# An RWKV-7 and attention stack on one core: early decay products, gate blocks inside the group norm's wait, two output blocks side by side

## The chip, the cores and the metric

The kernel runs on one core of one Trainium2 chip, in one launch. The time is device microseconds of one execution. The kernel before was run three times: median 2448.25 us, from 2446.24 to 2455.63.

## What is computed

Two transformer blocks over 512 tokens of width 1024. The change touches only the first layer, RWKV-7 time mixing, which in the reference is this:

```python
rkv = jnp.einsum('pbtd,pde->pbte', jnp.stack([x_r, x_k, x_v]), w_rkv)
r, k, v = rkv[0], rkv[1], rkv[2]
w = -jax.nn.softplus(-(w0 + jnp.tanh(x_w @ w1) @ w2)) - 0.5
decay = jnp.exp(-jnp.exp(w.astype(f32)))
a = jax.nn.sigmoid(a0 + (x_a @ a1) @ a2)
g = jax.nn.sigmoid(x_g @ g1) @ g2
kk = to_heads((k * k_k).astype(f32))
kk = kk / jnp.maximum(jnp.linalg.norm(kk, axis=-1, keepdims=True), 1e-12)
k = k * (1.0 + (a - 1.0) * k_a)
...
# a scan over the tokens with r, decay, k, v, kk and kk * a gives y
...
mean = jnp.mean(y, axis=-1, keepdims=True)
var = jnp.mean(jnp.square(y - mean), axis=-1, keepdims=True)
y = (y - mean) * lax.rsqrt(var + GN_EPS)
y = y.reshape(B, T, D) * lnx_w.astype(f32) + lnx_b.astype(f32)
bonus = jnp.sum(r_h * k_h * r_k.astype(f32), axis=-1, keepdims=True) * v_h
y = (y + bonus.reshape(B, T, D)).astype(h.dtype) * g
return y @ w_o
```

After it come an MLP, a forgetting-attention layer, a second MLP, and a second block with sparse attention, a convolution and a third MLP. None of these is edited.

## The kernel before

**Tiling.** Activations lie transposed, as 8 tiles of 128 features x 512 tokens. Weights come as blocks of 128 x 1024 in one stream (raw, four buffers). GpSimd (POOL) splits each block into a rounded high part and a remainder (whi, wlo, two slots each); a product is three matmuls, high x high, high x low and low x high, so a block is 8 x 3 = 24 matmuls of 128 x 512. There is no scheduler: each engine's program is written out by hand, and semaphores order the engines. The semaphore blk counts the weight blocks that TensorE is through with, split_ready those that POOL has split. POOL splits block b as soon as blk reaches b - 1.

**Preparation of the scan.** TensorE computes k, r and v in blocks 6 to 29. After each of the first v blocks e stands a group of head sums (BETWEEN: the norm of kk after e = 0 and 1, the bonus sums "bo" two by two after e = 2 to 5), and after e = 3 to 6 two matmuls kk_spread, which spread the inverse norms (rows kkR) over the features. VectorE (DVE) makes the products in place: the bonus product r * r_k * k into tmpA and tmpB in turn (L1902), then, for each tile, the normed kk (L1919), kk * a (L1920) times the inverse decay RD (L1921), kk times the shifted decay (L1924), r times the decay DEC (L1930), k times RD (L1931). ScalarE (ACT) reads the v blocks and turns them over. Then TensorE transposes k, b = kk * a and v (tokens, L706), and matmuls L743 spread the bonus sums. The scan itself runs in 4 turns of 128 tokens and is bound to the engines' mutual waits.

**Group norm, gates and output.** When the scan is done, TensorE takes the means (L1001), DVE subtracts them (L2064), ACT squares (L1539), TensorE sums the squares by head (head_sum, L618), ACT takes the root and DVE the inverse (L2013, L2016, L1906). Only then begins a loop over 8 tiles e: a matmul spreads the inverse deviation (L631), 6 matmuls make the gate tile from sgH and sgL with the two gate_up blocks, DVE multiplies (L2069), ACT applies lnx_w and lnx_b (L1544), DVE adds the bonus BON (L2073), multiplies with the gate in PSUM (L2080), ACT rounds to YH (L1547), DVE subtracts to YL (L2084). After the loop, linear("rwkv_o") computes 8 output blocks of 24 matmuls; the first waits tile by tile for y_lo. The blocks of rwkv_o come after the two gate_up blocks in the stream, so POOL splits the first of them when gate tile 7 has released its slot. The stream itself stops before rwkv_o until the scan is done, since X is loaded again first (rec_done).

The lines at the places that the change touches:

```python
for e in range(DT):
    spread("gn", e, [2, 3], gnR)
    if e >= 2:
        pe.wait_ge(S("y_gated"), e - 1)
    mm = three(ps[:, 6 + e % 2, :], (g0 % SPL, e), sgH[:, 0, :], sgL[:, 0, :], True, False)
```

## Time and profile before

| what | value |
|---|---|
| median of three runs | 2448.25 us |
| the profiled execution: its own time | 2456.9 us |
| its span (first to last instruction) | 2455.1 us |
| TensorE busy | 2356.1 us (96%) |
| VectorE busy | 1185.8 us (48%) |
| ScalarE busy | 573.3 us (23%) |
| GpSimd busy | 1288.6 us (52%) |
| mean granted TensorE clock | 0.975 |

The profiled execution took 1.8 us more than its span, and 8.65 us more than the median of the runs. Time on the trace counts from the span's start. The preparation of the scan that the change rewrites lies at 153 to 252 us, the group norm, gates and output at 448 to 548 us. PE in a row is TensorE's matmul, DVE VectorE, ACT ScalarE, POOL GpSimd. KR in a row is one tensor that holds both r (Rr) and kk (KN), ps is PSUM, ssq also the scan's state; tmpA and tmpB are the two work tiles. A granted clock of 1.00 is 2.4 GHz, 0.50 is 1.2 GHz.

### The profile page before, as it was taken

The numbers are of one execution on the slowest core, as the hardware profiler recorded it, in microseconds if no ns is written. First come the engines' busy times: TensorE is split into PE (matmuls) and PEld (weight loads), VectorE is DVE, ScalarE is ACT, GpSimd is POOL, SyncE is SP. The second block draws the span as 40 slices with busy tenths as digits, with TensorE's granted clock in tenths as the row PEclk, the third lists the DMA queues.
The fourth block names the chain that finished last, engine by engine and source line by source line (L and its number), as shares of the span: only waits on it lengthen the run. The fifth ranks groups of instructions, "written<-read, shape, count | busy, mean of one in ns | idle before, by whom it ended". The sixth has DMA issues, their size and how long they took to land.

```text
span 2455.1 us, 41848 instructions
## 1 busy us (share of the span) xinstructions
PE 2356.1 (96%) x16922; PEld 1886.6 (77%) x16922; DVE 1185.8 (48%) x1476; ACT 573.3 (23%) x1168; POOL 1288.6 (52%) x839
## 2 busy tenths in 40 slices
PE   8998999899999999989999999999999998999999
PEld 5765888578888877667788888787877777888887
DVE  8857433474343462566544333518045656633433
ACT  4542333221110122144311011101015541201100
POOL 5642001066666665455566666566645445666665
PEclk9998999789999999999999999999999989999999
DMA  4220000122222222200222322233221112222322
GB/s 152 86 69 18 3 3 3 70 77 95 96 101 94 94 91 75 82 27 34 71 95 95 102 94 94 89 100 126 95 79 44 44 35 69 95 95 96 101 94 86
DMA packets 50447, 188.37 MB, mean 77 GB/s; under 512 B 5616, under 2 KB 5744, under 8 KB 49808
## 3 DMA queue, kind: packets, MB, share of 16 engines
q1 hardware_dynamic: 49824, 183.40, 22.3%
q10 hardware_dynamic: 496, 3.12, 0.3%
q8 instruction: 99, 1.62, 0.3%
q14 instruction: 28, 0.23, 0.0%
HBM read 184.33 MB, written 2.10 MB: 76 GB/s over the span
## 4 chain that ended last, share of the span: by engine, by line
PE 85%; DVE 10%; issue 2%; ACT 1%; POOL 1%; DMA 0%; ACTq 0%; DVEq 0%; SPq 0%; POOLq 0%
PE ps L606 23%; PE ps L608 22%; PE ps L607 22%; PE ps L1109 2%; PE ps L1124 2%; PE ps L793 2%; PE ps L618 2%; DVE HL L1993 1%; PE ps L1090 1%; PE ps L803 1%; PE ps L1091 1%; PE ps L801 1%; PE ps L786 1%; PE ps L779 1%; PE ps L631 1%
## 5 line engine op out<-in xcount | busy, mean ns | idle before, releaser
L448 POOL TENSOR_TENSOR wlo<-raw,whi 128x1024 fp32r<-128x1024 f32 (+1 forms) x354 | 825.6, 2332 | 26.4
L441 POOL TENSOR_SCALAR whi<-raw 128x1024 fp32r<-128x1024 f32 x335 | 361.1, 1078 | 808.6 <-PE ps L608 796.5
L606 PE MATMUL ps<-HH,whi 128*128 128x512 f32 x1312 | 529.8, 404 | 8.3 <-DVE HL L1993 8.3
L608 PE MATMUL ps<-HH,wlo 128*128 128x512 f32 x1312 | 514.4, 392 | 0.0
L607 PE MATMUL ps<-HL,whi 128*128 128x512 f32 x1312 | 514.1, 392 | 0.0
L606 PEld LDWEIGHTS ps<-HH,whi 128*128 128x128 f32 x1312 | 248.2, 189 | 70.0 <-DVE HL L1993 14.1
L607 PE MATMUL ps<-hidL,whi 128*128 128x512 f32 x768 | 298.8, 389 | 0.0
L606 PE MATMUL ps<-hidH,whi 128*128 128x512 f32 x768 | 298.8, 389 | 0.0
L608 PE MATMUL ps<-hidH,wlo 128*128 128x512 f32 x768 | 298.8, 389 | 0.0
L608 PEld LDWEIGHTS ps<-HH,wlo 128*128 128x128 f32 x1312 | 248.3, 189 | 52.8
L607 PEld LDWEIGHTS ps<-HL,whi 128*128 128x128 f32 x1312 | 248.6, 190 | 52.2 <-issue 4.3
L2040 DVE TENSOR_TENSOR X<-X,ps 128x512 f32<-128x512 f32 x192 | 123.3, 683 | 306.7 <-PE ps L608 306.7
L1511 ACT ACTIVATE sqrT<-relT 128x512 f32<-128x512 f32 x96 | 60.8, 634 | 792.0 <-DVE relT L2029 792.0
L2032 DVE TENSOR_TENSOR hidL<-sqrT,hidH 128x512 fp32r<-128x512 f32 x96 | 184.1, 1936 | 88.8 <-ACT hidH L1515 88.8
L2029 DVE SCALAR_TENSOR_TENSOR relT<-ps,rstd 128x512 f32<-128x512 f32 x96 | 66.4, 691 | 234.1 <-PE ps L608 234.0
L606 PEld LDWEIGHTS ps<-hidH,whi 128*128 128x128 f32 x768 | 144.2, 188 | 29.9
L607 PEld LDWEIGHTS ps<-hidL,whi 128*128 128x128 f32 x768 | 144.2, 188 | 29.9
L608 PEld LDWEIGHTS ps<-hidH,wlo 128*128 128x128 f32 x768 | 144.2, 188 | 29.8
L478 POOL TENSOR_TENSOR mRB<-mRB,cst 128x512 f32<-128x512 f32 x8 | 10.1, 1279 | 174.3 <-ACT mRB L1465 174.3
L507 POOL TENSOR_SCALAR prs<-prs,cls,GT 128x32 f32<-128x32 f32 (+4 forms) x48 | 32.9, 686 | 79.7 <-DVE cls L2167 67.8
L606 PE MATMUL ps<-mixH,whi 128*128 128x512 f32 x128 | 52.4, 409 | 10.8 <-DVE mixL L1849 8.8
L1335 ACT ACTIVATE HH<-X,vec 128x512 fp32r<-128x512 f32 x40 | 28.8, 721 | 143.1 <-DVE X L2000 70.3
(445 smaller groups left out, 3598.4 us busy)
## 6 DMA issues: line engine op xcount, KB each, us to landing
raw<-stream SPq DMA_DIRECT2D x336, 512.0 KB, 3.3
X<-xT SPq DMA_DIRECT2D x2, 1024.0 KB, 6.7
X<-xT SPq DMA_DIRECT2D x1, 2048.0 KB, 7.9
CW<-cmpw ACTq DMA_DIRECT2D x1, 2048.0 KB, 9.5
out<-X SPq DMA_DIRECT2D x4, 512.0 KB, 2.7
cst<-consts SPq DMA_DIRECT2D x1, 511.5 KB, 9.3
c2f<-consts ACTq DMA_DIRECT2D x1, 466.0 KB, 3.0
c2s<-consts ACTq DMA_DIRECT2D x1, 466.0 KB, 4.1
```

The source lines that it names most:

```text
L441: pool.tensor_scalar(hi, raw[:, j, :].rearrange("p (k m) -> p k m", k=DT), 1.0, 0.0, ALU.mult, ALU.add)\
L448: return pool.tensor_tensor(wlo[:, s, a:z, :], raw[:, j, a * P:z * P].rearrange("p (k m) -> p k m", k=z - a), whi[:, s, a:z, :].bitcast(F3 ...
L606: pe.matmul(acc, whi[:, s, k, :], hi, start=start, stop=False)
L607: pe.matmul(acc, whi[:, s, k, :], lo, start=False, stop=False)
L608: return pe.matmul(acc, wlo[:, s, k, :], hi, start=False, stop=stop)
L618: pe.matmul(ps[0:112, bank, :], gather_heads(i), tmp[i % 2][:, :], start=i == 0, stop=i == n - 1).then_inc(S(f"{tag}_sum"), 1)
L793: mm = pe.matmul(square(hp, 1 - c, hp, p), mN[half(c), hp, p, :], mT[half(c), hp, p, :], start=True, stop=True)
L1109: mm = pe.transpose(ps[0:w, 4 + hp, j * P:(j + 1) * P], B["P"][:, 2 * (u % 2) + hp, j * P:j * P + w], ident)
L1511: act.activation(sqrT[:, j % 2, :], relT[:, j % 2, :], ACT.Square).then_inc(S("full"), 1)
L2029: dve.scalar_tensor_tensor(relT[:, j % 2, :], ps[:, j, :], 0.0, rstd[:, :], ALU.max, ALU.mult).then_inc(S("rel"), 1)
L2032: dve.tensor_tensor(hidL[buf][:, j - 1, :], sqrT[:, (j - 1) % 2, :], hidH[buf][:, j - 1, :].bitcast(F32), ALU.subtract).then_inc(S("hid"), 1)
L2040: ins = dve.tensor_tensor(X[:, e, :], X[:, e, :], ps[:, 4 + 2 * (j % 2) + o, :], ALU.add)
```

## The change

Three parts.

**Early decay products.** A new buffer bon holds the bonus products of tiles 0 to 5 (6 and 7 go to tmpA and tmpB), so they need not wait for the head sums before them. A function decayed(i) makes, as soon as tile i of r is read, the bonus product, -a * RD, r * DEC and k * RD; tiles 0 to 5 stand ahead of the inverse norms of kk, tiles 6 and 7 behind them. The sign of kk moves into k_k. Of the loop over kk_spread three operations for each tile stay. ACT's first copy of the turned tokens also waits for kn.

**Group norm and gates.** lnx_b is added to BON by ACT during the scan (two tiles at the start of each turn). Means use four banks and alternate with head sums. Gate tiles 0 to 4 stand directly behind the head sums, ahead of the first spread; ACT copies each gate tile to a new buffer G in SBUF. DVE applies lnx_w together with the inverse deviation, so that ACT's affine step goes. DVE's y_lo moves ahead of the bonus sum.

**Two output blocks side by side.** Blocks 0 and 1 of rwkv_o are split into buffers of their own (oH, oL, in the place of kk), from the end of the scan on. TensorE takes them together, tile by tile: as soon as y_lo of tile k is there, 6 matmuls (y_apart). Gate tiles 5 to 7 and spreads 3 to 7 stand between them. Blocks 2 to 7 follow.

```diff
-                if not isinstance(b, int) or b >= 2 * RAW:
+                if not isinstance(b, int) or b >= 2 * RAW and not 0 <= b - START["rwkv_o"] < 4:
                     pool.wait_ge(S("blk"), b - (SPL - 1))
+                elif b - START["rwkv_o"] in (0, 1):
+                    pool.wait_ge(S("rec_done"), 1)
+                elif b - START["rwkv_o"] in (2, 3):
+                    pool.wait_ge(S("blk"), START["rwkv_o"])
...
+            pe.wait_ge(S("y_done"), NCH)
+            for i in range(DT + 3):
+                if i < DT:
+                    if i >= 4:
+                        pe.wait_ge(S("gn_c"), i - 3)
+                    pe.matmul(ps[:, i % 4, :], const("bones"), Rr[:, i, :], start=True, stop=True).then_inc(S("gn_mean"), 1)
+                if i >= 3:
+                    head_sum("gn", i - 3, DT)
...
+            def y_apart(e, k):
+
+                acc = ps[:, e, :]
+                pe.matmul(acc, oH[:, e, k, :], YH[:, k, :], start=k == 0, stop=False)
+                pe.matmul(acc, oH[:, e, k, :], YL[:, k, :], start=False, stop=False)
+                mm = pe.matmul(acc, oL[:, e, k, :], YH[:, k, :], start=False, stop=k == DT - 1)
+                if k == DT - 1:
+                    mm.then_inc(S("blk"), 1)
+
+            SPREADS = [2, 3, 5]
+            for e in range(5):
+                gate_tile(e)
+            pe.wait_ge(S("gn_c"), DT)
+            for i in range(3):
+                spread("gn", i, SPREADS, gnR)
+            for k in range(DT):
+                if k + 5 < DT:
+                    gate_tile(k + 5)
+                if k + 3 < DT:
+                    spread("gn", k + 3, SPREADS, gnR)
+                if k == 0:
+                    ready(y0 + 1)
+                pe.wait_ge(S("y_lo"), k + 1)
+                for e in range(2):
+                    y_apart(e, k)
...
             for n in range(QT):
+                act.wait_ge(S("bo_used"), DT)
+                for i in (2 * n, 2 * n + 1):
+                    mark(act.activation(BON[:, i, :], BON[:, i, :], ACT.Identity, bias=vcol("lnx_b", i)), "bias_added")
...
+            for e in range(5):
+                gate_read(e)
+            for i in range(DT):
+                if i + 5 < DT:
+                    gate_read(i + 5)
+                act.wait_ge(S("y_gated"), i + 1)
+                mark(act.activation(YH[:, i, :], tmp[i % 2][:, :], ACT.Copy), "y_hi")
...
+            def decayed(i):
+                dve.wait_ge(S("rkv_read"), 8 + i + 1)
+                product = bon[:, i, :] if i < 6 else tmp[i - 6][:, :]
+                mark(dve.scalar_tensor_tensor(product, Rr[:, i, :], vcol("r_k", i), Kk[:, i, :], ALU.mult, ALU.mult), "bo_sq")
+                mark(dve.scalar_tensor_tensor(AG[:, i, :], AG[:, i, :], -1.0, RD[:, i, :], ALU.mult, ALU.mult), "kn_rest")
+                dve.wait_ge(S("bo_sq"), i + 1)
+                mark(dve.tensor_tensor(Rr[:, i, :], Rr[:, i, :], DEC[:, i, :], ALU.mult), "rt")
+                mark(dve.tensor_tensor(Kk[:, i, :], Kk[:, i, :], RD[:, i, :], ALU.mult), "kt")
...
-            bonus(0)
-            bonus(1)
+            for i in range(6):
+                decayed(i)
             dve.wait_ge(S("kk_norm"), 1)
...
-            bonus(2)
-            bonus(3)
+            decayed(6)
+            decayed(7)
             for i in range(DT):
                 dve.wait_ge(S("kk_spread"), i + 1)
                 link(dve.tensor_tensor(KN[:, i, :], KN[:, i, :], ps[:, 6 + i % 2, :], ALU.mult), "kk_used")
-                link(dve.tensor_tensor(AG[:, i, :], AG[:, i, :], KN[:, i, :], ALU.mult))
-                mark(dve.tensor_tensor(AG[:, i, :], AG[:, i, :], RD[:, i, :], ALU.mult), "bt")
+                dve.wait_ge(S("kn_rest"), i + 1)
+                mark(dve.tensor_tensor(AG[:, i, :], AG[:, i, :], KN[:, i, :], ALU.mult), "bt")
...
+                dve.wait_ge(S("bt"), i + 1)
+                mark(dve.tensor_tensor(a[:, :, 1:C], a[:, :, 1:C], d[:, :, 0:C - 1], ALU.mult), "kn")
...
+            dve.wait_ge(S("gn_c"), DT)
+            dve.wait_ge(*count("bias_added", DT))
             for n in range(DT + 2):
                 if n < DT:
                     dve.wait_ge(*count("gn_spread", n + 1))
-                    mark(dve.tensor_tensor(Rr[:, n, :], Rr[:, n, :], ps[:, 2 + n % 2, :], ALU.mult), "gn_used")
...
+                    mark(dve.scalar_tensor_tensor(Rr[:, n, :], Rr[:, n, :], vcol("lnx_w", n), ps[:, (2, 3, 5)[n % 3], :], ALU.mult, ALU.mult), "gn_used")
```

On DVE, ahead of the inverse norms of kk, before the change. Rows name line, operation, output and inputs, width, and the semaphores waited for; kk_norm is the root of the norms by ACT:

```order
98 L1902 SCALAR_TENSOR_TENSOR tmpA<-KR,vec,Kk 128x512 [waits kk_sum,dve_chain]
99 L1902 SCALAR_TENSOR_TENSOR tmpB<-KR,vec,Kk 128x512 [waits kk_sum]
100 L1911 TENSOR_SCALAR rstd<-rstd 112x512 [waits kk_norm]
101 L1912 RECIPROCAL rstd<-rstd 112x512 [waits dve_chain]
102 L1913 CAST kkR<-rstd 112x512 [waits dve_chain]
```

The same place of the changed kernel, from the last of the six early tiles on:

```order
118 L1976 TENSOR_TENSOR Kk<-Kk,RD 128x512
119 L1972 SCALAR_TENSOR_TENSOR bon<-KR,vec,Kk 128x512 [waits rkv_read]
120 L1973 SCALAR_TENSOR_TENSOR AG<-AG,RD 128x512
121 L1975 TENSOR_TENSOR KR<-KR,DEC 128x512 [waits bo_sq]
122 L1976 TENSOR_TENSOR Kk<-Kk,RD 128x512
123 L1985 TENSOR_SCALAR rstd<-rstd 112x512 [waits kk_norm]
124 L1986 RECIPROCAL rstd<-rstd 112x512 [waits dve_chain]
125 L1987 CAST kkR<-rstd 112x512 [waits dve_chain]
```

24 operations on whole tiles now stand between the copy of the decays and the inverse norms, where two stood, and they wait for the reads of r, not for sums.

On TensorE, behind the head sums of the group norm, before (heads_root is the inverse deviation, heads_sq a square):

```order
1569 L618 MATMUL ps<-tmpB,cst 112x512 [waits heads_sq]
1570 L631 MATMUL ps<-gnR,pselR 128x512 [waits heads_root,sg_split,split_ready]
1571 L606 MATMUL ps<-sgH,whi 128x512
1572 L607 MATMUL ps<-sgL,whi 128x512
1573 L608 MATMUL ps<-sgH,wlo 128x512
```

And in the changed kernel, the end of gate tile 4 and what follows:

```order
1598 L623 MATMUL ps<-sgH,whi 128x512
1599 L624 MATMUL ps<-sgL,whi 128x512
1600 L625 MATMUL ps<-sgH,wlo 128x512
1601 L648 MATMUL ps<-gnR,pselR 128x512 [waits heads_root,gn_c]
1602 L648 MATMUL ps<-gnR,pselR 128x512 x2
1603 L623 MATMUL ps<-sgH,whi 128x512 [waits gn_aff]
...
1609 L648 MATMUL ps<-gnR,pselR 128x512 [waits heads_used]
1610 L1045 MATMUL ps<-YH,oH 128x512 [waits y_lo,split_ready]
1611 L1046 MATMUL ps<-YL,oH 128x512
1612 L1047 MATMUL ps<-YH,oL 128x512
```

30 gate matmuls (1571 to 1600) moved ahead of the wait for the inverse deviation, and the output matmuls for tile 0 now stand behind gate tile 5, ahead of gate tiles 6 and 7.

On DVE, one step of the gated output before, and then one step of the changed kernel:

```order
231 L2069 TENSOR_TENSOR KR<-KR,ps 128x512 [waits heads_spread]
232 L2073 TENSOR_TENSOR KR<-KR,BON 128x512 [waits gn_aff]
233 L2080 TENSOR_TENSOR tmpA<-KR,ps 128x512 [waits y_hi,gate_up,dve_chain]
234 L2084 TENSOR_TENSOR YL<-tmpB,YH 128x512 [waits y_hi]
```

```order
229 L2139 SCALAR_TENSOR_TENSOR KR<-KR,vec,ps 128x512 [waits heads_spread]
230 L2143 TENSOR_TENSOR YL<-tmpB,YH 128x512 [waits y_hi]
231 L2147 TENSOR_TENSOR KR<-KR,BON 128x512 [waits heads_used]
232 L2151 TENSOR_TENSOR tmpA<-KR,G 128x512 [waits y_lo,gn_aff,dve_chain]
```

Four operations stay four. The sum with BON no longer waits for ACT, the gate comes from SBUF (G) where it came from PSUM, and gn_aff is now ACT's copy of the gate tile.

## Rows read from the trace of the kernel before

**Rows 1.** The page: the chain of work that ended last, by engine.

```profile
PE 85%; DVE 10%; issue 2%; ACT 1%; POOL 1%; DMA 0%; ACTq 0%; DVEq 0%; SPq 0%; POOLq 0%
```

**Rows 2.** Waits of TensorE, 150 to 560 us: total us, times, longest.

```profile
PE ps L631 <- DVE gnR L1906: 6.2, 1, 6.2
PE ps L618 <- DVE tmpB L1902: 5.1, 1, 5.1
PE ps L706 <- DVE boR L1906: 4.7, 1, 4.7
```

**Rows 3.** Stretches: length, busy us of PE, PEld, DVE, ACT, POOL; granted clock; DMA.

```profile
200.00:205.00 5.00, 1.89 (x2) 0.45 (x2) 4.86 (x7) 0.00 (x0) 1.18 (x1) 0.51 0.01 3
...
455.00:460.00 5.00, 5.00 (x12) 1.72 (x12) 1.99 (x3) 1.56 (x3) 0.00 (x0) 1.00 0.95 387
...
465.00:470.00 5.00, 0.00 (x0) 0.00 (x0) 4.89 (x4) 0.00 (x0) 0.00 (x0) 0.64 0.00 0
...
480.00:498.00 18.00, 18.00 (x36) 10.55 (x36) 12.99 (x21) 7.21 (x10) 0.00 (x0) 0.50 0.00 1
```

**Rows 4.** Timeline of TensorE, v blocks: start, us, idle before it.

```profile
197.01 1.02 PE L618 MATMUL ps<-tmpA,cst 128*112 128x512 f32 x2
203.11 2.05 PE L618 MATMUL ps<-tmpB,cst 128*112 128x512 f32 x2 [5.08 <-DVE tmpB L1902]
...
234.25 5.35 PE L706 MATMUL ps<-cst,Kk 128*128 128x128 f32 x32 [4.68 <-DVE boR L1906]
...
243.11 0.49 PE L743 MATMUL ps<-boR,pselR 48*128 48x512 f32 x1
```

**Rows 5.** Timeline of VectorE, the same stage.

```profile
176.56 0.75 DVE L1902 SCALAR_TENSOR_TENSOR tmpA<-KR,vec,Kk 128x512 f32<-128x512 f32 x1 [16.92 <-PE ps L618]
...
182.20 4.35 DVE L1906 TENSOR_TENSOR kkR<-rstd,kkR 16x512 fp32r<-16x512 f32 x2
...
199.01 2.71 DVE L1921 TENSOR_TENSOR AG<-AG,RD 128x512 f32<-128x512 f32 x1
...
232.74 1.41 DVE L1906 TENSOR_TENSOR boR<-ps,boR 16x512 fp32r<-16x512 f32 x2
```

**Rows 6.** Timeline of GpSimd: one split.

```profile
197.40 1.04 POOL L441 TENSOR_SCALAR whi<-raw 128x1024 fp32r<-128x1024 f32 x1 [4.52 <-PE ps L608]
198.52 2.65 POOL L448 TENSOR_TENSOR wlo<-raw,whi 128x1024 fp32r<-128x1024 f32 x1
```

**Rows 7.** Timeline of ScalarE: reads of r, copies of the turned tokens.

```profile
153.56 5.38 ACT L1381 ACTIVATE KR<-ps 128x512 f32<-128x512 f32 x8 [1.01 <-PE ps L608]
...
240.29 4.08 ACT L1452 ACTIVATE Btok<-ps 128x512 f32<-128x512 f32 x8
```

**Rows 8.** Timeline of TensorE: group norm, gates, output, start of the MLP.

```profile
463.23 1.02 PE L618 MATMUL ps<-tmpB,cst 128*112 128x512 f32 x2
470.40 0.76 PE L631 MATMUL ps<-gnR,pselR 48*128 48x512 f32 x1 [6.15 <-DVE gnR L1906]
...
477.52 0.79 PE L631 MATMUL ps<-gnR,pselR 48*128 48x512 f32 x1
...
501.96 0.77 PE L606 MATMUL ps<-YH,whi 128*128 128x512 f32 x1 [2.88 <-issue]
...
510.05 0.39 PE L606 MATMUL ps<-YH,whi 128*128 128x512 f32 x1
...
548.13 0.39 PE L606 MATMUL ps<-HH,whi 128*128 128x512 f32 x1
```

**Rows 9.** Timeline of VectorE: steps of the gated output, and its last row.

```profile
478.36 0.69 DVE L2069 TENSOR_TENSOR KR<-KR,ps 128x512 f32<-128x512 f32 x1 [1.57 <-PE ps L631]
478.96 0.68 DVE L2073 TENSOR_TENSOR KR<-KR,BON 128x512 f32<-128x512 f32 x1
...
480.28 0.68 DVE L2084 TENSOR_TENSOR YL<-tmpA,YH 128x512 fp32r<-128x512 f32 x1
...
503.82 2.79 DVE L2084 TENSOR_TENSOR YL<-tmpB,YH 128x512 fp32r<-128x512 f32 x1
```

More of the change, by code:

```diff
@@ L993, in mlp @@
                 down(base + 60, 7, 1, last=True)
-            g0 = START["gate_up"]
-            for i in range(DT):
-                pe.wait_ge(S("y_done"), NCH)
-                if i >= 2:
-                    pe.wait_ge(S("gn_c"), i - 1)
-                pe.matmul(ps[:, i % 2, :], const("bones"), Rr[:, i, :], start=True, stop=True).then_inc(S("gn_mean"), 1)
-            head_sums("gn", DT)
-            ready(g0 + 1)
-            pe.wait_ge(S("sg_split"), 1)
-            for e in range(DT):
-                spread("gn", e, [2, 3], gnR)
-                if e >= 2:
-                    pe.wait_ge(S("y_gated"), e - 1)
-                mm = three(ps[:, 6 + e % 2, :], (g0 % SPL, e), sgH[:, 0, :], sgL[:, 0, :], True, False)
+            pe.wait_ge(S("y_done"), NCH)
@@ L1016, in _ @@
+            pe.wait_ge(*count("gn_used", DT))
+            for e in range(2, DT):
+                ready(y0 + e)
+                if e >= 4:
+                    pe.wait_ge(S("x_up"), e - 3)
+                for k in range(DT):
+                    mm = three(ps[:, e % 4, :], ((y0 + e) % SPL, k), YH[:, k, :], YL[:, k, :], k == 0, k == DT - 1)
+                mm.then_inc(S("blk"), 1)
             mlp(0, 1, HH, HL)
```

97 lines of the change are left out of this document (53 added, 44 removed).

## The prediction, on record before the changed kernel ran

> **What bounds the kernel now.** I read the chain of waits first: 85% of it is TensorE [rows 1], so most of the kernel is matmul after matmul and this change cannot touch it. The list of TensorE's waits then shows where the first layer is not: three waits of 6.2, 5.1 and 4.7 us, all for VectorE, and all in the two stretches that the diff rewrites [rows 2]. The table of stretches adds a second loss: the granted clock is 0.51 around the 5.1 us wait, falls to 0.64 in the 6.15 us one, and is 0.50 through the whole gate loop [rows 3], though TensorE there shows as busy 18.00 of 18.00 us. So each long wait is paid twice, as a wait and as matmuls at 1.2 GHz behind it. The reader should see from the timelines that in the v blocks TensorE waits for a product that VectorE could have made long before (VectorE idled 16.92 us ahead of 176.56, though r was being read from 153.56 on) [rows 5, 7], and that in the gate loop every tile costs (477.52 - 470.40) / 2 = 3.56 us [rows 8].
>
> **First part, the preparation.** On TensorE from 197.01 to 234.25 stand three v blocks, four bonus sums, six spreads, and the waits [rows 4]. A block of 24 matmuls at full clock takes (548.13 - 510.05) / 7 = 5.44 us [rows 8], three are 16.3; a bonus sum is about 0.88 (its row says 1.02 for a pair of matmuls that overlaps the next by its drain [rows 4]), four are 3.5; six spreads at 0.36, my estimate from the 0.49 of such a row, are 2.2. Sum 22.0, so without waits the transposes start at 219.05, not at 234.25: 15.2 us less. That needs VectorE to be in time at two places.
>
> The inverse norms of kk come first. VectorE now has 24 tile operations ahead of them. It starts at about 154.3, when the first tile of r is read [rows 7]. A tile operation takes about 0.64 us from start to start (the rows at 478.36 and 478.96 stand 0.60 apart, a scalar_tensor_tensor is 0.75 long) [rows 5, 9], together 15.3. But the same rows show that an operation whose inputs both lie in SBUF waits for a POOL operation under way: 2.71 us at 199.01, until 0.55 after POOL's end at 201.17, and 4.35 for two small rows at 182.20 [rows 5, 6]. All 24 are of that kind. Four splits of 1.04 + 2.39 us fall into this stretch (the second half is 2.65 when one VectorE operation slips in between [rows 6]). Walking them through in turn, I get 3 to 4 operations between the first splits, 8 in the long gap up to 173, and the last done at 181.3. The inverse (0.42 + 3.35 + 0.43 + two small rows of 0.70, about 5.8 us with its links) ends at 187.1. TensorE asks for it after v block 3 and two sums, which is one block and two spreads ahead of 197.01 [rows 4], at 190.8. Slack 3.7 us, so I cost the move at nothing; without that cover each microsecond late would be one of TensorE's. The second place is the loop over kk_spread: three operations for a tile, about 2.05 us, where five to eight stood, so that VectorE is through with tile 7 at 217.6 and with the bonus rows (1.41) [rows 5] at 219.0, just when TensorE ends its last v block. The 4.7 us wait goes; what is late next is nothing by more than 0.2 us.
>
> The transposes: 64 of them took 243.11 - 234.25 = 8.86 us [rows 4], the first 32 at a clock that was still recovering. Then ACT's copies bound them, 4.08 / 8 = 0.51 us each [rows 7]. The last v read ends at 220.1 (219.05, 0.4 of drain, one copy), TensorE's last group follows the twelfth copy, 220.1 + 12 x 0.51 + 0.6 = 226.8; so 7.7 us from 219.05, a further 1.2 gained. Everything up to the scan is paced as before. ACT's new wait for kn (217.6) holds only that first copy, which is later anyway. First part: **-16.4 us**; bounds -17.5 (the copies start with the transposes) and -11 (one lock more on the way, a wait of some 3 us and half clock behind it).
>
> The two bias activations at the head of each turn of the scan are 0.5 to 0.7 us each by the nearest ACT passes over a tile [rows 7]. I cost them at nothing: ACT waits there for VectorE's masking of the first products. Without that cover the copy to mRB is late, at the worst by 1.4 us in three turns.
>
> **Second part, group norm and gates.** Means and sums are 16 products of about 0.88 us. Before, with two banks, the last sum began at 463.23 [rows 8]; interleaved from 447.83 on with one short wait for the first square, it ends at 462.2 instead of 464.25: -2.0. The chain root, inverse, cast and rows stays 6.15 us long, so the inverse deviation is there at 468.3. Gate tiles 0 to 4, 6 matmuls of 0.227 us each (5.44 / 24) or 1.36 us a tile, fill 462.1 to 468.9. The wait of 6.2 us is covered, and with it the reason for the low clock: tiles cost 1.36 where the loop took 3.56.
>
> Then VectorE paces. A step is 2.53 us of its own time (478.36 to 480.28 plus 0.61) [rows 9] and about 2.7 with the wait for ACT's rounding. But for tiles 0, 1 and 2 there is a ring: gate tile k+5 on TensorE, ACT's copy of it, which stands ahead of ACT's rounding of tile k, VectorE's y_lo, y_apart, the next gate tile: 1.36 + 0.4 + 0.6 + 0.6 + 0.75 + 1.36, about 5 us. That gives y_lo of tile 0 at 473.4 and tile 1 at 478.4. At 481.4 gate tile 7 is done and blk reaches 32: POOL now splits blocks 34 and 35, 6.9 us of locks, in the middle of the steps. VectorE's sum, gate product and y_lo all read two SBUF tensors; before, the gate came from PSUM, and POOL came only at the last steps (2.79 us at 503.82 [rows 9]). I get y_lo of tile 2 at 485.3 and of tile 3 at 491.1, then 2.73 each, tile 7 at 502.1, y_apart done at 503.5.
>
> The Trainium skill, page "SBUF — State Buffer", section "Who interferes with whom", says that a VectorE instruction with two SBUF inputs contends with a GpSimd instruction that reads SBUF and that the loser fully blocks; by it the new gate operand is a cost, and without it the sum would be 4 us better. The 2.71 and 2.79 us rows agree with it.
>
> Blocks 32 and 33 cost POOL nothing on the path: the X load and the stream keep the DMA queues at 0.95 until 460 [rows 3], POOL splits them by 465 to 467, and they are asked for at 472. Blocks 2 to 7 are 6 x 5.44 = 32.7 us: the MLP starts at 536.2 instead of 548.13 [rows 8]. Second and third part: **-11.9 us**, bounds -16.5 (no lock in steps 2 and 3) and -7.
>
> **Sum.** -16.4 - 11.9 = -28.3 us. The profiled execution took 2456.9 (span 2455.1) and would take 2428.6; the median lies 8.65 below it, at 2448.25, so the forecast is 2420.
>
> **The rivals.**
> Clock falls again. TensorE idles about 3.9 us ahead of y_lo 2, and 3.9 again ahead of y_lo 3. Waits of 4.68 and 5.08 us had half clock behind them [rows 3, 4]; none of 3.9 is there to read. If it falls, steps stay paced by VectorE (2.6 us of matmuls in 2.73), but the last y_apart takes 1.3 more, and blocks 2 on start at half clock, as the first output block did before: 510.05 - 501.96 = 8.1 instead of 5.44, so 2.6. Together +3.9: 2424.
> The Trainium skill, page "TensorE: Matmul & The Clock Gate", section "HAM oscillation — how this bites in real kernels", describes this: bursts with waits between them, each starting throttled. It speaks for this rival.
> The locks miss. POOL and VectorE ask within 0.1 us of each other ahead of y_lo 2; if VectorE gets in first, steps 2 and 3 gain about 4 us and TensorE never idles long: 2416.
> Inverse norms late. If the 24 operations meet the locks worse, by more than 3.7 us, TensorE waits ahead of v block 4, some 3 us plus 3 of half clock, and the loop behind slips: +6 to +8, 2427. For it: 24 operations against 8 POOL instructions. Against: the 16.92 us of idleness that they go into.
> The output blocks gain nothing. If y_lo keeps the old 3.56 us pace, tile 7 comes at 507 to 508 and the last term is worth 5 us less: 2425.
> Slower than before. The clock falls at 482 and does not recover in the run of output blocks. 24 matmuls at half clock last 10.3 us (0.43 each), six blocks cost 29 more, with the 1.3 above about +30.5: 2450. It decides from 5.6 blocks at half clock on. Before, the first output block took 8.1 us where half clock throughout would be 10.3, so the clock came back within it, which speaks against this rival.
>
> **How the numbers follow.** A measurement of this kernel can tell about 0.5% (12.2 us) from no change. Chances: forecast 0.40, clock falls 0.24, locks miss 0.10, inverse norms late 0.12, old pace 0.07, slower rival 0.02, and 0.05 for what I have not seen, spread over all sides. The cases from 2416 to 2427, each some 4 us wide because the runs before lie within 9.4 us, give 2412 to 2431. Faster by over 0.5% (below 2436): 0.93; within: 0.05; slower: 0.02.
>
> **What would show it.** In the profile after: no wait of TensorE over 1 us between 165 and 235, clock 1.00 there; transposes starting near 219; the scan starting at 236; kk's inverse norms before 190.8. Later, 16 us earlier than the times above: gate tiles right behind the last sum at clock 1.00; y_lo of tile 2 up to 2.4 us long; two TensorE waits of about 4 us for YL; the MLP starting near 520. I am wrong if a wait for kkR stands ahead of v block 4, or if the six output blocks take over 36 us.

## The result, and the profile after

| kernel | median us | lowest to highest | executions |
|---|---|---|---|
| before | 2447.67 | 2446.24 to 2455.63 | 4 |
| changed | 2427.66 | 2425.18 to 2428.23 | 4 |

The ratio is 0.9911, 95% interval 0.9893 to 0.9929: 20.0 us less, faster by more than the 0.5% that this measurement can tell from no change. The profiled execution of the changed kernel took 2427.87 us with a span of 2426.0, which is 29.1 less than the span of before. These two differences, 20.0 and 29.1, are the first thing to explain, and the stages are the way to do it.

The list of TensorE's waits from 140 to 560 us, in the form of [rows 2], now reads so:

```profile
PE ps L1045 <- DVE YL L2143: 10.2, 5, 4.9
PE ps L789 <- issue: 2.2, 3, 1.6
PE ps L623 <- DVE mixL L1919: 2.0, 1, 2.0
```

The three waits of [rows 2] are gone. What stands in their place is one group for YL, five waits with 10.2 us together, the longest 4.9. The chain of the page, beside [rows 1]:

```profile
PE 87%; DVE 8%; issue 2%; ACT 2%; POOL 1%; DMA 0%; ACTq 0%; DVEq 0%; SPq 0%; POOLq 0%
```

VectorE's share fell from 10 to 8%. The timeline of TensorE in the preparation, beside [rows 4]:

```profile
164.93 1.02 PE L635 MATMUL ps<-tmpA,cst 128*112 128x512 f32 x2
...
190.33 1.88 PE L635 MATMUL ps<-bon,cst 128*112 128x512 f32 x4
192.14 0.72 PE L731 MATMUL ps<-kkR,pselR 48*128 48x512 f32 x2
...
220.79 3.68 PE L723 MATMUL ps<-cst,Kk 128*128 128x128 f32 x32
...
228.17 0.49 PE L763 MATMUL ps<-boR,pselR 48*128 48x512 f32 x1
...
237.16 1.98 PE L799 MATMUL ps<-KR,AG 64*64 64x128 f32 x64 [0.84 <-issue]
```

No row of this stretch carries a wait for VectorE. The transposes start at 220.79 where they started at 234.25. The first 32 take 3.68 us where they took 5.35, so the clock is up when they begin, as the stretches say:

```profile
165.00:190.00 25.00, 25.00 (x92) 16.41 (x91) 24.83 (x25) 7.25 (x11) 12.79 (x6) 1.00 0.26 84
190.00:205.00 15.00, 15.00 (x57) 9.96 (x56) 14.76 (x16) 1.20 (x2) 8.05 (x4) 1.00 0.10 37
205.00:235.00 30.00, 30.00 (x161) 22.10 (x161) 18.41 (x28) 11.91 (x23) 3.79 (x2) 1.00 0.00 1
```

TensorE is busy for 70.00 of 70.00 us at a granted clock of 1.00 (its upper level). In the first of these stretches VectorE is busy for 24.83 of 25.00 us, where it worked for 11.26 of them before. Its timeline, beside [rows 5]:

```profile
155.62 2.88 DVE L1972 SCALAR_TENSOR_TENSOR bon<-KR,vec,Kk 128x512 f32<-128x512 f32 x1 [2.25 <-ACT KR L1440]
...
180.90 0.68 DVE L1976 TENSOR_TENSOR Kk<-Kk,RD 128x512 f32<-128x512 f32 x1
...
181.96 3.35 DVE L1986 RECIPROCAL rstd<-rstd 112x512 f32<-112x512 f32 x1
185.34 1.99 DVE L1987 CAST kkR<-rstd 112x512 fp32r<-112x512 f32 x1
187.36 1.40 DVE L1980 TENSOR_TENSOR kkR<-rstd,kkR 16x512 fp32r<-16x512 f32 x2
```

The 24 early operations end at 181.5, the inverse norms at 188.76. TensorE asks for them at 192.14: they are 3.4 us early.

In the output, TensorE's timeline beside [rows 8]:

```profile
433.39 3.70 PE L1021 MATMUL ps<-KR,cst 128*128 128x512 f32 x8 [0.69 <-ACT KR L1551]
...
446.80 1.02 PE L635 MATMUL ps<-tmpB,cst 128*112 128x512 f32 x2
...
454.60 0.96 PE L648 MATMUL ps<-gnR,pselR 48*128 48x512 f32 x3
...
464.40 0.50 PE L1045 MATMUL ps<-YH,oH 128*128 128x512 f32 x1 [1.51 <-DVE YL L2143]
...
465.97 0.63 PE L623 MATMUL ps<-sgH,whi 128*128 128x512 f32 x1
...
477.65 0.80 PE L1045 MATMUL ps<-YH,oH 128*128 128x512 f32 x1 [4.91 <-DVE YL L2143]
...
522.64 0.39 PE L623 MATMUL ps<-HH,whi 128*128 128x512 f32 x1
```

The old 6.15 us wait ahead of the first spread is filled with gate tiles. The waits have moved into the steps: the longest are 1.51 us ahead of 464.40 and 4.91 ahead of 477.65; the other three are 1.96, 1.26 and 0.57 us. The stretches show what the clock made of them:

```profile
446.00:456.00 10.00, 10.00 (x39) 6.98 (x40) 5.91 (x6) 4.31 (x7) 3.71 (x3) 1.00 0.33 105
456.00:466.00 10.00, 6.53 (x26) 4.39 (x26) 7.54 (x12) 2.34 (x4) 0.00 (x0) 0.99 0.01 2
466.00:472.00 6.00, 4.74 (x14) 2.95 (x12) 2.42 (x3) 1.12 (x2) 2.96 (x2) 0.73 0.00 0
472.00:478.00 6.00, 1.09 (x4) 0.53 (x3) 5.92 (x5) 0.63 (x1) 4.96 (x3) 0.84 0.26 87
478.00:486.00 8.00, 8.00 (x18) 5.56 (x18) 7.13 (x12) 1.89 (x3) 0.00 (x0) 0.50 0.18 66
486.00:492.00 6.00, 5.43 (x23) 4.14 (x22) 3.97 (x7) 2.34 (x4) 0.00 (x0) 0.98 0.00 0
```

The five gate tiles ahead of the first spread run at 1.00. The clock falls a first time behind the waits of 1.96 and 1.51 us: the matmul at 465.97 takes 0.63 us where it took 0.39, and the mean over 466 to 472 is 0.73. From 478 to 486 the clock is 0.50, its lower level, and it is back at 0.98 behind. What TensorE waits for is in VectorE's timeline, beside [rows 9]:

```profile
458.66 0.69 DVE L2143 TENSOR_TENSOR YL<-tmpA,YH 128x512 fp32r<-128x512 f32 x1
...
463.65 0.69 DVE L2143 TENSOR_TENSOR YL<-tmpB,YH 128x512 fp32r<-128x512 f32 x1 [2.32 <-ACT YH L1617]
...
469.92 0.69 DVE L2143 TENSOR_TENSOR YL<-tmpA,YH 128x512 fp32r<-128x512 f32 x1 [3.58 <-ACT YH L1617]
470.53 2.87 DVE L2147 TENSOR_TENSOR KR<-KR,BON 128x512 f32<-128x512 f32 x1
...
475.54 2.06 DVE L2143 TENSOR_TENSOR YL<-tmpB,YH 128x512 fp32r<-128x512 f32 x1
...
487.76 0.69 DVE L2143 TENSOR_TENSOR YL<-tmpB,YH 128x512 fp32r<-128x512 f32 x1 [0.70 <-ACT YH L1617]
```

Two things stretch the steps. First, VectorE waits 2.32 and 3.58 us for ACT's rounding, and ACT itself had been waiting for a gate tile:

```profile
462.51 0.60 ACT L1609 ACTIVATE G<-ps 128x512 f32<-128x512 f32 x1 [3.88 <-PE ps L625]
463.00 0.62 ACT L1617 ACTIVATE YH<-tmpB 128x512 fp32r<-128x512 f32 x1
```

This is the ring of the prediction: TensorE makes gate tile 6 behind the output matmuls of step 0, ACT copies it before it rounds tile 1, and step 1 of TensorE needs that rounding. Second, a sum takes 2.87 us instead of 0.68 and a y_lo 2.06 instead of 0.69, while GpSimd splits two blocks (these waits of VectorE for GpSimd are called locks here):

```profile
468.96 1.05 POOL L454 TENSOR_SCALAR whi<-raw 128x1024 fp32r<-128x1024 f32 x1 [19.17 <-PE ps L625]
470.09 2.76 POOL L461 TENSOR_TENSOR wlo<-raw,whi 128x1024 fp32r<-128x1024 f32 x1
```

**The difference by stage.** The preparation goes from the first head sum of kk to the scan's first matmul, the output from the first mean to the first matmul of the MLP. For the profiled execution of before the borders are 163.59, 252.11, 447.83 and 548.13.

| kernel | first sum at | preparation | scan | output | rest | span |
|---|---|---|---|---|---|---|
| before | 163.59 | 88.52 | 195.72 | 100.30 | 1906.97 | 2455.1 |
| changed | 164.93 | 72.23 | 196.23 | 89.25 | 1903.36 | 2426.0 |
| difference | +1.34 | -16.29 | +0.51 | -11.05 | -3.61 | -29.1 |

The two stages that the diff edits give 27.34 of the 29.1 us. The rest, behind the MLP's start, is 3.61 us shorter, though the change doesn't touch it; the later first sum and the scan take 1.85 back.

### The profile page after: what moved, and what is told of

It is laid out like the page before. It is cut to its first block, busy times and chain, and to the rows that moved or that the text cites. A ratio compares the mean times of both kernels' runs of the same rounds, so it can differ in the third digit from the quotient of the medians.

```text
span 2426.0 us, 41845 instructions
## 1 busy us (share of the span) xinstructions
PE 2339.6 (96%) x16922; PEld 1878.7 (77%) x16922; DVE 1190.7 (49%) x1469; ACT 576.1 (24%) x1176; POOL 1293.8 (53%) x839
## 4 chain that ended last, share of the span: by engine, by line
PE 87%; DVE 8%; issue 2%; ACT 2%; POOL 1%; DMA 0%; ACTq 0%; DVEq 0%; SPq 0%; POOLq 0%
PE ps L623 23%; PE ps L624 23%; PE ps L625 23%; PE ps L1168 2%; PE ps L1183 2%; PE ps L813 2%; PE ps L635 2%; DVE HL L2061 1%; PE ps L1149 1%; PE ps L1150 1%; PE ps L823 1%; PE ps L821 1%; PE ps L806 1%; DVE ssq L1845 1%; PE ps L799 1%
```

## The experiments

Twelve kernels ran, in three groups of four, each group on one chip beside the kernel before, which ran 17, 9 and 8 times there: medians 2453.37, 2453.45 and 2453.50. Each ratio is to the runs of the same group. The changed kernel itself ran only in the first group (after_again), so the later kernels are compared with it across chips. Stage lengths come from one profiled execution of each kernel. Excerpts of diffs are against the changed kernel, and dots mark what is left out.

### The two kernels again

**before_again** and **after_again** are the two kernels with no edit.

> The kernel before, unchanged, to settle why the profiled execution took 29 us less after the change (span 2455.1 to 2426.0) and the medians only 20 us less. Theory: the profiled execution of before was a long one; its stage from 153 to 548 us is ordinary, and the surplus lies in stretches at half clock behind it. Then this profile shows the first MLP starting within 1.5 us of 548.1, a span near 2446, and about 5 us less of half-clock cost after 548. Rival: the stage itself was long in that execution; then the MLP starts near 542.5 here and the rest is as long as before (1907 us). Time: 2447, ratio 1.000.

> The changed kernel, unchanged. Theory: the MLP starts at 522.6 within 1.5 us, and what is behind it lasts 1903 us within 4, where half clock falls elsewhere from execution to execution. Rival: what is behind the MLP's start is steadily 5 us longer than in the kernel before, because other phases of the clock meet other waits. Time 2427, 20 us less than before.

Before: 2453.37 (2446.90 to 2458.22, 12 executions), ratio 1.0002, 0.9988 to 1.0015. Changed: 2429.85 (2429.34 to 2430.36), ratio 0.9902, 0.9888 to 0.9917. So before has a spread of 12 us, and a median of three can lie anywhere in it: of the 17 executions beside this job, 4 took 2446.2 to 2448.6, at a granted clock over the whole span of 0.981 or 0.982, the other 13 took 2452 to 2459. Of the 34 executions of the three groups, 7 took under 2449 us; of the four behind the result above, 3 did. Their low median was thus in good part luck, though that their chip had a share in it isn't excluded. Where in the program the short executions save their time wasn't seen: the two profiled ones of before took 2456.9 and 2452.51 us. The forecast of 2447 for before_again leaned on the low median and was a miss. By stage the profile of before_again has 88.45, 196.65, 100.00 and a rest of 1902.07, after_again 72.21, 195.86, 91.00 and 1905.26. The edited stages repeat within 0.3 us in before and differ by 1.8 in the output of the changed kernel, which the part on the ring comes back to. The rest differs by 4.9 us between two executions of before alone, and over all 14 profiles, whatever the edit, it lies between 1901.1 and 1907.3. In the second pair it is 3.19 us longer in the changed kernel where it was 3.61 shorter in the first. So the 3.61 us above are within what executions differ by, and no sign of the change.

The first sum comes 0.74 to 1.34 us later in the two profiles of the changed kernel, and the stretch from 140 to 160 us shows a companion of it. First before_again, then after_again:

```profile
140.00:160.00 20.00, 18.01 (x80) 14.49 (x79) 12.79 (x13) 11.42 (x19) 10.43 (x7) 1.00 0.22 79
```

```profile
140.00:160.00 20.00, 18.01 (x73) 14.44 (x72) 16.71 (x18) 10.76 (x18) 8.76 (x6) 0.91 0.22 78
```

The same wait of 2.0 us for mixL stands in both, the busy time is the same 18.01, yet the clock is 1.00 in one and 0.91 in the other. Of the 14 profiles seven have 0.91 here and seven 1.00. The kernel with the output edits alone has 0.91, and four kernels of the sections below that do have the early products have 1.00 (round_first, early_splits, filled_wait and four_side_by_side, all on one chip), so the change doesn't decide it. The first sum comes at 163.94 to 165.05 with 0.91 and at 162.81 to 164.13 with 1.00. What decides the clock here stays open.

### One part at a time

**prep_only** keeps the early products and the order of the head sums, with group norm, gates and output as before. **output_only** is the converse: group norm, gates, bias activations and output as changed, the products and the order of the head sums as before.

```diff
 # prep_only
-            for i in range(DT + 3):
-                if i < DT:
-                    ...
-                if i >= 3:
-                    head_sum("gn", i - 3, DT)
...
+            for i in range(DT):
+                ...
+            head_sums("gn", DT)
...
+            linear("rwkv_o", YH, YL, ("y_lo", 0), ("x_up", 0), [])
 # output_only
-    bon = at("bon", [P, 6, T], zone(8, 4096))
...
-            def decayed(i):
...
```

> Only the first part: the early decay products, with bon, k_k negated and the shorter loop over kk_spread; group norm, gates and output as before. Theory: the part saves its 16.3 us of the trace, the scan starts at 236 to 237.5 and the MLP at 532; time 16 us less than before, 2431. Rival, that a good part of the traced gain does not arrive at the end (the medians moved by 20 and not 27): 11 to 12 us less, 2436.

> Only the second and third part: bias in the scan, four banks for the means, gate tiles ahead of the spreads, G in SBUF, output blocks 0 and 1 tile by tile; the preparation of the scan as before. Theory: from the first mean to the MLP's start 89.2 us where before has 100.3, the whole 11 us less, 2436. Rival, that the gain does not all arrive: 7 to 8 us less, 2440. The sum of this gain and that of the preparation alone should be that of the whole change within 4 us.

prep_only: 2438.20 (2437.05 to 2441.44), ratio 0.9940, 0.9927 to 0.9953, that is -15.2 us; preparation 72.23, output 100.04. output_only: 2442.82 (2441.38 to 2448.08), ratio 0.9957, 0.9944 to 0.9970, -10.6 us; preparation 88.71, output 91.13. Together -25.7, against -23.5 for both in one kernel: the parts add up within their intervals, and each acts in its own stage alone. The expected savings of 16 and 11 us came, and the times expected with them (2431 and 2436) were too low by the low median of before. The scan keeps its length, 196.61 in prep_only and 196.23 in the changed kernel with its bias activations: these cost nothing that shows.

### How far from late are the inverse norms

**late_kk_6** and **late_kk_12** put extra VectorE passes, whose result nothing reads, ahead of the inverse norms of kk.

```diff
+            for _ in range(6):
+                link(dve.tensor_tensor(ssq[:, :], RD[:, 0, :], DEC[:, 0, :], ALU.mult))
             dve.wait_ge(S("kk_norm"), 1)
```

> The changed kernel with 6 more VectorE passes (RD x DEC of tile 0 into a scratch tile, not read, linked one behind the other) ahead of the inverse norms of kk. Theory: the inverse norms are ready 3.4 us before TensorE asks for them (188.8 against 192.1). Six passes of 0.7 us and one lock more (about 2.8) make them 7 late, so TensorE waits 3 to 4 us ahead of v block 4, about 5 us with half clock behind it: 2434. Rival, that the slack is worth nothing to begin with or that the loop over kk_spread takes the delay up: 2429 or 2437.

> The same with 12 passes. Theory: the rows come 11 to 12 us later, TensorE waits 8 us ahead of v block 4 and works some microseconds at half clock: about 10 us over the changed kernel, 2439. That prices a preparation in which VectorE's early products meet too many locks. Rival: under 5 us, 2434, because the later waits of the preparation shrink by as much.

The passes of VectorE and the first spread of TensorE behind them, first with six, then with twelve:

```profile
180.80 7.11 DVE L1985 TENSOR_TENSOR ssq<-RD,DEC 128x512 f32<-128x512 f32 x6
...
191.79 1.93 DVE L1989 CAST kkR<-rstd 112x512 fp32r<-112x512 f32 x1
```

```profile
195.21 1.18 PE L731 MATMUL ps<-kkR,pselR 48*128 48x512 f32 x2 [3.75 <-DVE kkR L1980]
```

```profile
180.53 14.26 DVE L1985 TENSOR_TENSOR ssq<-RD,DEC 128x512 f32<-128x512 f32 x12
...
198.67 0.43 DVE L1989 CAST kkR<-rstd 112x512 fp32r<-112x512 f32 x1
```

```profile
200.58 1.22 PE L731 MATMUL ps<-kkR,pselR 48*128 48x512 f32 x2 [9.35 <-DVE kkR L1980]
```

7.11 less a slack of 3.4 is 3.7, and the wait is 3.75. 14.26 less 3.4 is 10.9, less the 1.5 that the cast no longer waits for GpSimd is 9.4, and the wait is 9.35. The slack is thus measured from the other side. The stage grows to 79.19 and 83.69, +7.0 and +11.5, that is the wait and some 3 or 2 us of half clock behind it: the granted clock from 190 to 205 is 0.77 and 0.66. The times are 2434.61 (2433.06 to 2437.27), ratio 0.9922, 0.9900 to 0.9944, and 2437.14 (2436.68 to 2443.62), ratio 0.9943, 0.9923 to 0.9962: 4.8 and 7.3 over after_again. The first was expected at 2434 and came; the second lies between its theory (2439) and its rival (2434). Why the medians grew less than the stages isn't settled; 2 to 4 us are within what executions differ by behind the MLP's start.

### The ring, the locks and the clock

**round_first** lets ACT round tile i before it copies gate tile i + 5. **early_splits** gives the output blocks 2 and 3 buffers of their own, loads them ahead of X, and lets GpSimd split them when the scan is done, so that no split falls into the steps. **filled_wait** puts 20 matmuls, whose result nothing reads, ahead of the wait of step 3.

```diff
 # round_first
-                if i + 5 < DT:
-                    gate_read(i + 5)
                 act.wait_ge(S("y_gated"), i + 1)
                 mark(act.activation(YH[:, i, :], ...), "y_hi")
+                if i + 5 < DT:
+                    gate_read(i + 5)
 # early_splits
+            APART[START["rwkv_o"] + 2 + e] = o2H[:, e, :, :], o2L[:, e, :, :]
...
+            rest(START["rwkv_o"], RAW)
             sp.wait_ge(S("rec_done"), 1)
...
-                elif b - START["rwkv_o"] in (0, 1):
+                elif b - START["rwkv_o"] in (0, 1, 2, 3):
                     pool.wait_ge(S("rec_done"), 1)
 # filled_wait
+                if k == 3:
+                    pe.wait_ge(S("gn_aff"), 8)
+                    for _ in range(20):
+                        pe.matmul(ps[:, 6, :], oH[:, 0, 0, :], YH[:, 0, :], start=True, stop=True)
                 pe.wait_ge(S("y_lo"), k + 1)
```

> The changed kernel with one edit: ACT rounds tile i to YH before it copies gate tile i+5, not after. Theory (the ring): y_lo of tiles 1 and 2 waits for gate tiles that TensorE makes only after the output matmuls of the tile before, so each of these steps costs 5 to 6 us instead of 2.7. Without the ring y_lo 1 and 2 come 2.7 to 3.2 us apart, POOL's two splits still fall into the steps behind, and from the first mean to the MLP's start it takes 85 us where the changed kernel takes 89 to 91: 5 us less than it, time 2425. Rival (the locks decide): the ring only moved the wait, the two splits come earlier and cost the same, gain under 2 us, 2428.

> The changed kernel with output blocks 2 and 3 also split into buffers of their own (zone 9), the four blocks loaded ahead of the X load and split from the end of the scan on; the ring stays, blocks 2 and 3 are still computed after 0 and 1. Theory (locks): no POOL work lies in the eight steps, so VectorE's operations of 2.87, 1.41 and 2.06 us go back to 0.7; y_lo 3 comes 4.5 us earlier, TensorE's wait of 4.9 us falls to 1.3 and the clock stays at 1.00: 84 us from the first mean to the MLP, 6 us less than the changed kernel, 2424. Rival: the splits now meet the chain of the inverse deviation (cast and two small rows) and cost there what they cost later, 2429.

> The changed kernel with 20 more matmuls (oH x YH into a free bank, not read) put into TensorE's longest wait, ahead of y_lo 3. Theory (clock): that wait of 4.9 us brings half clock, which costs 1.3 us on the last output tile and up to 2.6 on the block behind; filled, the clock stays 1.00 to the MLP and the stage ends 2 to 3 us earlier, 2427. Rival: VectorE paces the steps whatever the clock, and the clock is back before the last tile, so nothing moves: 2429 to 2430.

| kernel | median us | ratio, 95% | output stage |
|---|---|---|---|
| after_again | 2429.85 | 0.9902 (0.9888 to 0.9917) | 91.00 |
| round_first | 2420.81 | 0.9877 (0.9858 to 0.9897) | 83.71 |
| early_splits | 2421.51 | 0.9878 (0.9859 to 0.9897) | 85.19 |
| filled_wait | 2427.16 | 0.9903 (0.9886 to 0.9920) | 89.64 |

The executions of round_first (2418.34 to 2424.20) and early_splits (2420.56 to 2423.25) all lie below the eight of the changed kernel (2425.18 to 2430.36), though the intervals of the ratios touch. Without the ring, y_lo of tiles 0 to 3 start at 457.03, 459.75, 462.47 and 465.47, VectorE's own pace of 2.7 to 3.0 us apart, where they stood 5.0, 6.3 and 5.6 apart; the step behind is still 5.6 long, with a y_lo of 2.06 us: the locks. Without the locks, it is the other way round: the ring's steps of 6.4 and 5.0 us remain for tiles 0 to 2, and then all are 2.7. Against the 89.25 of the first profile the ring costs 5.5 us and the locks 4.1; against the 91.00 of the second 7.3 and 5.8.

The two profiles of the changed kernel differ just in the ring. From y_lo of tile 0 to that of tile 1 it takes 4.99 us in the first and 6.46 in the second, and TensorE's clock in this step makes the difference. The first profile, then after_again:

```profile
459.50:464.40 4.90, 3.39 (x13) 2.33 (x13) 2.55 (x5) 1.11 (x2) 0.00 (x0) 1.00 0.01 3
```

```profile
458.45:464.81 6.36, 4.86 (x13) 3.38 (x13) 2.54 (x5) 1.11 (x2) 0.00 (x0) 0.76 0.01 3
```

TensorE is busy for 1.47 us more, which is all of the difference: the 12 matmuls between one y_lo and the next, six of output and six of a gate tile, stand in the ring. The wait ahead of them is 1.96 us in both. The other kernels that keep ACT's order agree: a ring step takes 4.96 to 5.03 us where the clock is 1.00 and 6.27 to 6.60 where it is 0.73 to 0.77. The output stage goes with it, 89.25 to 89.64 us where the first ring step ran at 1.00 and 91.00 to 91.13 where it did not. So the short waits do cost through the clock, 1.3 to 1.6 us a ring step. The first profile and early_splits have one slow ring step each, so the 4.1 us of the locks compares like with like.

filled_wait kept the clock up where it was to, from 478 to 486, but not 10 us sooner. Its stretches:

```profile
466.00:472.00 6.00, 4.49 (x13) 2.74 (x12) 2.77 (x2) 1.11 (x2) 3.65 (x2) 0.78 0.00 0
...
478.00:486.00 8.00, 6.16 (x25) 4.02 (x24) 7.12 (x12) 1.90 (x3) 0.00 (x0) 1.00 0.12 50
```

With the clock at 1.00 instead of 0.50 in those 8 us the stage is 89.64, no shorter than 89.25. From y_lo of tile 3 to the MLP it takes 47.10 us in the first profile, 47.12 in after_again and 47.17 in filled_wait. TensorE was busy for 8.00 of them before and is for 6.16 now: VectorE sets the pace of these steps, and TensorE at half clock just keeps up. The half clock from 478 to 486 is a companion of the loss and not a cause; the low clock in the ring steps, ahead of the filled wait, this kernel didn't touch. Its time of 2427.16, though it is the 2427 of the theory, can't be told from that of after_again, and the stage went as the rival said.

### Both causes out, and four blocks side by side

**round_and_early** joins the first two. **four_side_by_side** has the early splits and computes output blocks 2 and 3 in the steps too, which leaves two PSUM banks for the gates and two for the spreads. **four_spreads_early** is the same with another order of VectorE's step, the sum first and the use of the spread last.

```diff
 # four_side_by_side, on top of early_splits and round_first
-            SPREADS = [2, 3, 5]
+            SPREADS = [4, 5]
...
-                if k + 3 < DT:
-                    spread("gn", k + 3, SPREADS, gnR)
+                if k + 2 < DT:
+                    spread("gn", k + 2, SPREADS, gnR)
...
                 pe.wait_ge(S("y_lo"), k + 1)
-                for e in range(2):
+                for e in range(4):
                     y_apart(e, k)
 # four_spreads_early, VectorE's turn n
 #   before: used(n), y_lo(n - 2), add(n - 1), gated(n - 1)
 #   now:    add(n - 1), y_lo(n - 2), gated(n - 1), used(n)
```

> Four output blocks side by side, with the early splits and ACT's rounding first; gates in banks 6 and 7, spreads in 4 and 5, output in 0 to 3; POOL splits blocks 4 and 5 behind gate tile 7. Theory: a step has 12 output matmuls, 2.72 us, as long as VectorE's 2.7, so TensorE never waits over 1 us and the clock stays 1.00; the steps take about 27 us from y_lo 0 and four blocks (21.8) remain: about 75 us from the first mean to the MLP where the changed kernel takes 89 to 91. Time 2415, 14 us less than the changed kernel, 38 less than before. Rival: the splits of blocks 4 and 5 fall into the steps and hold VectorE up by 5 us, 2420.

> Four output blocks side by side as before, but VectorE takes the sum with BON first, then y_lo of the tile before, the gate product, and the spread product last. In the first form each y_lo stood behind a spread product whose spread TensorE made only after the output matmuls of the step before, two banks being too few: steps of 5 to 8 us. Theory: now TensorE paces, 2.72 us of output matmuls, a spread (0.4) and in three steps a gate tile (1.36), about 28.5 us from y_lo 0 on, then four blocks: 77.5 us from the first mean to the MLP's start, where the changed kernel takes 89 to 91 and the first form 91.3. Time 2416. Rival: ACT's rounding and the two late splits hold the steps at 3.5 us or more, 81 us and 2419.

> Both edits on the changed kernel, two blocks side by side: ACT rounds first, and blocks 2 and 3 are split early into buffers of their own. Alone they took the stretch from the first mean to the MLP to 83.7 and 85.2 us from 89 to 91. Theory: ring and locks are two costs and add up, since with both gone nothing holds VectorE's steps of 2.7 us: 79.5 us, time 2417. Rival: they overlap, because the lock fell into a step that the ring stretched anyway: 83 us, 2420.

round_and_early: 2417.86 (2415.20 to 2419.66), ratio 0.9855, 0.9832 to 0.9879, the fastest of all. Its output stage is 79.41 and its clock 1.00 from 456 to 480 us. Against the first profile the two costs add up: 9.8 us from 89.25 with both gone, 5.5 and 4.1 one by one. Against the 91.00 of the second it is 11.6, and 7.3 and 5.8 one by one, so they add up within the 1.8 us by which the stage of one kernel differs. Its steps in VectorE's timeline:

```profile
458.75 0.69 DVE L2150 TENSOR_TENSOR YL<-tmpA,YH 128x512 fp32r<-128x512 f32 x1
461.46 0.69 DVE L2150 TENSOR_TENSOR YL<-tmpB,YH 128x512 fp32r<-128x512 f32 x1
...
478.01 0.69 DVE L2150 TENSOR_TENSOR YL<-tmpB,YH 128x512 fp32r<-128x512 f32 x1 [0.70 <-ACT YH L1622]
```

Seven steps take 19.3 us, 2.75 each, where the changed kernel's take 29.1.

four_side_by_side: 2427.96 (2425.76 to 2428.51), ratio 0.9899, 0.9880 to 0.9918, output stage 91.32. Expected were 2415 and a stage of 75 us, so this was a miss. The reason stands in VectorE's timeline:

```profile
464.70 0.75 DVE L2144 SCALAR_TENSOR_TENSOR KR<-KR,vec,ps 128x512 f32<-128x512 f32 x1 [5.20 <-PE ps L652]
...
472.57 0.75 DVE L2144 SCALAR_TENSOR_TENSOR KR<-KR,vec,ps 128x512 f32<-128x512 f32 x1 [5.19 <-PE ps L652]
```

With two spread banks in place of three, TensorE can write spread k + 2 only behind the output matmuls of step k - 1, and these wait for a y_lo that VectorE does after it has used a spread. With that order turned round, four_spreads_early takes 2419.60 (2416.13 to 2423.52), ratio 0.9858, 0.9834 to 0.9882, stage 81.75, as its rival said (81 us, 2419): most of the loss was this ring. Its stage is still 2.3 us longer than that of round_and_early, and the two times can't be told apart. Its y_lo come at 458.00, 460.71, 466.76, 471.51, 478.55. In the two steps from 460.71 on VectorE still waits 3.25 and 1.95 us for a spread, and in the one behind them GpSimd, which now splits blocks 4 and 5 from 469.77 to 477.96, stretches a y_lo to 2.76 us.

## Why the prediction came out as it did

**The stages came out as forecast, within 3 us.** The preparation was forecast at -16.4 us and gave -16.3 (-16.2 in the second pair). The output was forecast at -11.9 and gave -11.05 and -9.0. The steps, with the clock of before moved on to each stage's own start: transposes forecast at 219.05 + 1.34 = 220.4, seen at 220.79. The 24 operations done at 181.3 + 1.34 = 182.6, seen at 181.5. Inverse norms with a slack of 3.7, seen 3.4 from the rows and again from the two kernels with extra passes; there was some luck in this one, since the 24 operations were 1.1 us early and the inverse behind them took 7.3 us and not 5.8, its cast having waited for GpSimd. Last sum over at 462.2 - 14.4 = 447.8, seen 447.82. y_lo of tiles 0 to 3, less 14.4: forecast 459.0, 464.0, 470.9, 476.7, seen 458.66, 463.65, 469.92, 475.54, and tile 7 at 487.7 and 487.76. MLP at 521.8, seen 522.64. The bias activations cost nothing, and from the end of the last y_lo (488.45) to the MLP it is 34.2 us, the last products of the two blocks side by side included, so the six blocks stay under the 36 that would have said otherwise. The forecast times of y_lo read as its ends, since y_apart is done 1.4 us (its six matmuls) after 502.1, and those seen are its starts, 0.69 us earlier; so the last y_lo ended 0.75 us late, and block 2 began at 490.00 where 503.5 less 14.4 is 489.1. That is the 0.85 us by which the output term missed in the first profile. Of the signs, the y_lo with a lock came one tile later (tile 3, 2.06 us), and of the two waits of about 4 us only one, the other four being under 2.

**The step that was off is the last one, from the profiled execution to the median.** I took 8.65 us off because the profiled execution of before lay that far above the median of its three runs. But 34 executions have medians of 2453.4 and 2453.5: the three had a low median, and 5.1 of the 8.65 us were that. The sum of -28.3 taken from 2453.4 gives 2425.1, and the median was 2427.66 and 2429.85. So of the 7.7 us by which 2420 was too low, some 5.1 are the baseline. The rest is the output term, 0.9 to 2.9 us too large, of which 1.7 are the slower ring steps of after_again, and a first sum 0.7 to 1.3 us later than before, which I had left as it was. The part behind the MLP's start alone spreads by 6.2 us from profile to profile, so the difference can't be accounted for to the last microsecond. The range of 2412 to 2431 held the time.

**The rivals.** "Clock falls again" came about in its mechanism and not in its price: there are five waits, the longest of 4.9 us, instead of two of 3.9, and half clock from 478 to 486 (in after_again seven waits, the longest of 3.6). I had priced the fall at 3.9 us, on the last output tile and on block 2; the clock was back ahead of both, and filled_wait shows that the half clock in the steps costs nothing that can be measured. What did cost was a fall that I had not looked for, in the ring steps, 1.3 to 1.6 us each. The Trainium skill, page "TensorE: Matmul & The Clock Gate", section "HAM oscillation — how this bites in real kernels", warned of just such bursts with waits between; the trace agrees on the fall (0.50); where VectorE paces it leaves its price near nothing, and in the ring steps it does not. "Locks miss" fell: rows of 2.87 and 2.06 us show them. By the Trainium skill, page "SBUF — State Buffer", section "Who interferes with whom", a VectorE instruction with two SBUF inputs contends with a GpSimd instruction that reads SBUF, and the trace agrees: the sum, the gate product and the y_lo beside the two splits take 2.87, 1.41 and 2.06 us where they take 0.7. I had put 4 us on the new gate operand alone. All locks together are worth 4.1 to 5.8 us by early_splits, the gate product's own row is only 0.72 us too long, and the sum and y_lo had two SBUF inputs before as well. So 4 us is right for the locks and too much for the operand; no kernel tested the operand by itself. "Inverse norms late" fell, with 3.4 us to spare, and late_kk_6 shows its price had it come: +7.0 in the stage, where I had said +6 to +8, but +4.8 in the median. "Old pace" fell: the last steps are 2.71 us apart. The slower one fell: the clock was back at 0.98 from 486 on.

**What I didn't see** is that the ring I had counted at about 5 us a step, worth 5.5 to 7.3 us in all by round_first, was one line's order: ACT's copy of a gate tile that isn't needed for five steps stood ahead of a rounding that was needed at once.

## What to carry to other kernels

Cost a change stage by stage from one trace, but take the baseline from many executions: here the stages came out within 3 us, and the median of three was 5 us off. When a wait is filled with work from elsewhere, look for the ring that it makes (an engine that serves an early need and a late one from one queue serves the late one first if it is written first) and for GpSimd work that its earlier release drops among VectorE's operations; here these two kept back 10 us beside the 27 that the edited stages gained. Measure a slack from the other side, with passes that nothing reads: the wait behind them is their length less the slack.

## What the runs showed of the hardware that I had not expected

- A wait of 2.0 us on TensorE is followed by a stretch below full clock in seven of 14 profiles and not in the other seven, with 17.93 to 18.02 us of work in each: 0.91 against 1.00 over 20 us. Executions of the kernel before lie up to 12.5 us apart on one chip, at mean clocks from 0.974 to 0.982. That such stretches make up the difference would fit, but wasn't followed.
- A wait of 1.96 us ahead of the first output tile left the clock at 1.00 in the first profile of the changed kernel, and in after_again the same wait had matmuls of 0.63 us instead of 0.39 behind it. In the first profile these came behind the next wait, of 1.51 us. Half clock cost 1.3 to 1.6 us in a step where TensorE's matmuls stood in the ring, and nothing in the steps that VectorE paced.
- A GpSimd pass can be the one that is held up. With VectorE's operations back to back its first half of a split took 2.63 us instead of 1.05:

```profile
174.40 2.63 POOL L454 TENSOR_SCALAR whi<-raw 128x1024 fp32r<-128x1024 f32 x1 [4.97 <-PE ps L625]
```

  A waiting VectorE operation seems to get in between GpSimd's two halves: there are VectorE rows of 1.52 us (at 165.69 and 176.05 us), each across the border of the halves, with a row of 2.85 or 2.88 behind it.
- The cast of one SBUF tensor took 1.99 us at 185.34 beside a GpSimd pass and 0.43 in late_kk_12 with GpSimd idle, so it waited too, while the reciprocal ahead of it took 3.35 us in both.
